# Residual sums as products with a scaled identity, and row norms shared between VectorE and ScalarE, in a four-layer transformer kernel

## The reference

```python
x = _layer_norm(DEEPNORM_ALPHA * x + mix, ln1_g[layer], ln1_b[layer])
ffn = _swiglu(x, ffn_w_gate[layer], ffn_w_up[layer], ffn_w_down[layer])
x = _layer_norm(DEEPNORM_ALPHA * x + ffn, ln2_g[layer], ln2_b[layer])
```

## Time and profile before

| | us |
|---|---|
| runs | 1052.35, 1056.54, 1061.19 |
| median | 1056.54 |
| the profiled execution | 1058.84 |
| its span | 1057.0 |
| PE busy | 994.2 (94%) |
| DVE busy | 655.3 (62%) |
| ACT busy | 452.5 (43%) |
| POOL busy | 155.5 (15%) |

### The profile page before, as it was taken

One profiled execution on the slowest core, in us unless ns is written; L12 is line 12 of the kernel. 1 busy time (PEld: TensorE's weight loads), 2 busy tenths in 40 slices (PEclk: granted clock), 3 DMA queues, 4 the chain that ended last, 5 costly groups with the idle time before them and its releaser, 6 DMA issues.

```text
span 1057.0 us, 15082 instructions
## 1 busy us (share of the span) xinstructions
PE 994.2 (94%) x5704; PEld 825.6 (78%) x5704; DVE 655.3 (62%) x1157; ACT 452.5 (43%) x689; POOL 155.5 (15%) x130
## 2 busy tenths in 40 slices
PE   5999989887999989999999999999999999999995
PEld 3899655676887668987788888878998778888884
DVE  4546453774674666655775766667446486766666
ACT  2253443632444623665334444443436334444441
POOL 3006001300691321140001000000006000000000
PEclk9999898998999999999999999999999999999998
DMA  9963354333553445321267544533533234654441
GB/s 376 351 241 136 123 197 159 121 120 130 188 197 141 163 178 196 130 82 47 113 225 252 219 179 179 189 145 137 198 128 121 84 124 167 243 197 179 179 179 40
DMA packets 23669, 178.40 MB, mean 169 GB/s; under 512 B 3743, under 2 KB 4175, under 8 KB 7111
## 3 DMA queue, kind: packets, MB, share of 16 engines
q1 hardware_dynamic: 19408, 166.70, 42.8%
q0 software_dynamic: 2224, 8.94, 2.5%
q10 hardware_dynamic: 1991, 2.14, 0.6%
HBM read 176.72 MB, written 1.05 MB: 168 GB/s over the span
## 4 chain that ended last, share of the span: by engine, by line
PE 83%; DVE 10%; DMA 4%; ACT 2%; issue 1%; POOL 0%; SPq 0%; DVEq 0%; ACTq 0%; POOLq 0%
PE G L958 14%; PE G L960 13%; PE G L959 13%; PE S L1062 7%; PE T L1062 7%; PE S L1061 3%; PE T L1061 3%; PE T L588 3%; PE T L483 2%; DVE wlo L1855 2%; PE G L407 1%; PE S L981 1%; PE G L604 1%; DMA ring<-in_ada_w 1%; PE G L602 1%; PE G L603 1%
## 5 line engine op out<-in xcount | busy, mean ns | idle before, releaser
L1972 DVE TENSOR_TENSOR wlo<-ring,whi 128x1024 fp32r<-128x1024 f32 (+1 forms) x90 | 154.5, 1722 | 91.3 <-ACT whi L1603 52.5
L958 PE MATMUL G<-whi,hTh 128*128 128x512 f32 (+3 forms) x560 | 199.9, 357 | 6.1 <-DVE hTl L524 3.4
L959 PE MATMUL G<-wlo,hTh 128*128 128x512 f32 (+3 forms) x544 | 187.6, 345 | 0.0
L960 PE MATMUL G<-whi,hTl 128*128 128x308 f32 (+3 forms) x496 | 168.7, 340 | 0.0
L1855 DVE TENSOR_TENSOR wlo<-ring,whi 128x1024 fp32r<-128x1024 f32 (+3 forms) x76 | 120.8, 1628 | 76.8 <-ACT whi L1498 76.5
L1062 PE MATMUL S<-hT,whi 128*128 128x512 f32 x352 | 128.1, 398 | 1.1 <-DVE wlo L1972 1.1
L1062 PE MATMUL T<-hT,whi 128*128 128x512 f32 x352 | 126.4, 394 | 0.0
L958 PEld LDWEIGHTS G<-whi,hTh 128*128 128x128 f32 x560 | 106.6, 190 | 20.1 <-DVE hTl L524 5.6
L1498 ACT CAST whi<-ring 128x1024 fp32r<-128x1024 f32 (+3 forms) x76 | 87.8, 1205 | 78.1 <-PE G L960 36.3
L959 PEld LDWEIGHTS G<-wlo,hTh 128*128 128x128 f32 x544 | 103.5, 190 | 9.3 <-issue 1.9
L960 PEld LDWEIGHTS G<-whi,hTl 128*128 128x128 f32 x496 | 94.1, 190 | 6.0
(11 more groups left out here) (334 smaller groups left out, 1762.8 us busy)
## 6 DMA issues: line engine op xcount, KB each, us to landing
ring<-in_ffn SPq DMA_DIRECT2D x44, 1536.0 KB, 6.4
ring<-in_ada_w SPq DMA_DIRECT2D x16, 1024.0 KB, 5.6
ring<-in_dil_w_in SPq DMA_DIRECT2D x16, 1024.0 KB, 4.8
ring<-in_cd_w_in SPq DMA_DIRECT2D x10, 1232.0 KB, 5.4
ring<-in_nsa_w_in SPq DMA_DIRECT2D x8, 1432.0 KB, 10.9
early<-in_ada_w SPq DMA_DIRECT2D x8, 1024.0 KB, 17.3
ring<-in_ab_w_in SPq DMA_DIRECT2D x4, 1440.0 KB, 6.2
vec<-in_vecs POOLq DMA_DIRECT2D x11, 512.0 KB, 5.2
```

Source lines behind the costliest of these rows:

```text
L958: pe.matmul(out_, act_h, w_h, start=first_, stop=False)
L959: pe.matmul(out_, act_h, w_l, start=False, stop=False)
L960: return pe.matmul(out_, act_l, w_h, start=False, stop=last_)
L1972: TT(wlo[b][:, part], ring[:, b, part], whi[b][:, part].bitcast(F32), ALU.subtract).then_inc(st[sig or what + "_lo"], 1)
```

## The change

All that follows is one change; nothing of what is computed is left out.

- **Residual of layers three and four.** In `project_out`, before the first weight item of a tile, PE puts ALPHA * x into that tile's two banks (`resid`), in place of one `keep_busy` product. DVE no longer adds; it takes the statistics from the banks, and the centring reads the banks in two halves.
- **First gate and up product.** It is made once for each token tile (`first_gate_up`): 32 passes of 256 columns, low weights against both parts of the activations. Tile 0's stands where four `keep_busy` products stood, and both `residual` products stand behind the transposes of tile 1.
- **Norms of layers one and two.** ACT squares the new x with a sum over the row (`row_squares`); DVE's three or four statistics instructions of a tile become one.
- **Norm after the feed-forward part.** Tile 1's mean and variance come from ACT, which reads the banks (`row_mean`, `row_spread`), while DVE works on tile 0.
- **Order.** The `late` blocks of layer one stand at p = 2, 5, 7, 9, 11, 12, the compressed products at 6, 8, 10, 13; the seventh `late` block stands before layer two's attention and the eighth at p = 2. The second weight item's low part of layer one's output is made in halves at p = 15 and before the last gate product. Layer two's second input item is multiplied with tile 0 before the transposes of tile 1. The three table loads wait for the 7th, 10th and 13th step of the first feed-forward part. POOL adds three branches before the last compressed sum. The scaled identity is made once, in another place (`cb`).

```diff
-        OUT_AT, LATE_AT, LATE_DIL = (6, 7, 10, 11), (2, 3, 5, 8, 9, 12), (2, 4)
+        OUT_AT, LATE_AT, LATE_DIL = (6, 8, 10, 13), (2, 5, 7, 9, 11, 12), (-1, 2)
...
+            if name in ("f0", "f1"):
+                return (TB[0], TB[1], S[1], TB[1])[g]
...
-            add_branch(1)
+            for q in range(1, 4):
+                add_branch(q)
             add_compressed(3)
-            for q in range(2, H // 2):
+            for q in range(4, H // 2):
                 add_branch(q)
...
-            for lo, base in ((0, P), (P, 0), (2 * P, P)):
+            for n, (lo, base) in enumerate(((0, P), (P, 0), (2 * P, P))):
+                pool.wait_ge(ffn[0]["act_ready"], 7 + 3 * n)
                 pool.dma_start(b8[:, :, lo:lo + P], bass.AP(tensor=rev.tensor, offset=base, ap=[[1, P], [rev.shape[1], 8], [1, P]])).then_inc(ck_loaded, 16)
...
+            def first_gate_up(name, st, t):
+
+                pe.wait_ge(*turned_tile(name, t))
+                pe.wait_ge(st["gu_lo"], 1)
+                for part, bank in enumerate((S[0], TB[0])):
+                    dst = bank[:, t * 2 * P:(t + 1) * 2 * P].rearrange("p (h c) -> p h c", h=2)
+                    for k in range(KT):
+                        at = slice((part * KT + k) * P, (part * KT + k + 1) * P)
+                        pe.matmul(dst, whi[0][:, at], hT2[:, k, :, t * P:(t + 1) * P], start=(k == 0), stop=False)
+                        ins = pe.matmul(dst, wlo[0][:, at], hT2[:, k, :, t * P:(t + 1) * P], start=False, stop=(k == KT - 1))
+                    if t == 1:
+                        ins.then_inc(st["gu_full"], 1)
+
...
-                gate_up(0, 0, True)
...
-                                             late_half == 0 and k == 0, late_half == 1 and k == OUT_K - 1)
+                                             i < 2 and late_half == 0 and k == 0, late_half == 1 and k == OUT_K - 1)
...
+                def resid(t):
+
+                    if i >= 2:
+                        pe.wait_ge(alpha_set, 1)
+                        for half in range(2):
+                            pe.matmul(G[OUT_BANK[half][t]][:], alpha_ident, x[:, t, half * 512:(half + 1) * 512], start=True, stop=False)
 
                 if not early:
                     turn_half(i, 0, *half_ready)
-                keep_busy(1, G[3])
+                if i < 2:
+                    keep_busy(1, G[3])
+                resid(0)
                 item(0, 0, 1).then_inc(used, 1)
                 pe.wait_ge(*all_ready)
+                resid(1)
                 if i == 1:
                     pe.wait_ge(shared_ready, 2)
...
+            dil_item(1, 1, 0, 0).then_inc(st["full"], 1)
             turn_pe(pe, "h1", norm_tiles(1), 1)
-            dil_item(1, 1, 0, 0).then_inc(st["full"], 1)
...
+            late_parts(pe, LATE_NSA, G[3])
             turn_pe(pe, "dil_rot", lambda g: pe.wait_ge(dil_s["rot_ready"], g + 1))
+            late_full(pe, LATE_NSA, G[3])
...
+                if p == 0:
+                    pe.wait_ge(late["taken"], LATE_NSA + 1)
...
+            first_gate_up("f0", ffn[0], 0)
+            turn_pe(pe, "f0", norm_tiles(5), 1)
             residual(0, 0, 11)
-            keep_busy(4)
-            turn_pe(pe, "f0", norm_tiles(5), 1)
             residual(0, 1, 12)
-            pe.wait_ge(*turned_all("f0"))
+            first_gate_up("f0", ffn[0], 1)
             ffn_pe("ffn0", ffn[0])
...
                 if name == "cd_in":
-                    high(name, 0, 1, KT * w)
+                    row_mean("ffn0")
                 turn_act(sc_e, turn_name, 0)
                 if name != "cd_in":
                     high(name, 0, 1, KT * w)
+                if name in ("dil_in", "ab_in"):
+                    row_squares(("dil_in", "ab_in").index(name), 1)
+                elif name == "cd_in":
+                    high(name, 0, 1, KT * w)
+                    row_spread(0)
                 turn_act(sc_e, turn_name, 1)
...
+            def row_squares(i, t):
+
+                sc_e.wait_ge(norm["resid"], 4 * i + 2 * (t + 1))
+                sc_e.activation(u[:, 0, 2 * D:3 * D], x[:, t, :], ACT.Square, scale=1.0 / 32, accum_out=var[:, t:t + 1]).then_inc(norm["squared"], 1)
+
+            def row_mean(name):
+
+                sc_e.wait_ge(used, split0[name] + FF_STEPS)
+                for half in range(2):
+                    ins = sc_e.activation(tok[:, 1, half * 512:(half + 1) * 512], G[2 + half][:], ACT.Copy, scale=1.0 / D,
+                                          accum_out=squares[:, half:half + 1])
+                ins.then_inc(norm["meaned"], 1)
+
+            def row_spread(i):
+
+                sc_e.wait_ge(norm["mean"], i + 1)
+                for half in range(2):
+                    ins = sc_e.activation(tok[:, 1, half * 512:(half + 1) * 512], G[2 + half][:], ACT.Square, scale=-1.0, bias=mv[:, 1, 0:1],
+                                          accum_out=squares[:, 2 + half:3 + half])
+                ins.then_inc(norm["squared"], 1)
+
...
+                if i < 2:
+                    row_squares(i, 0)
...
+            def squared_var(i, t):
+
+                dve.wait_ge(norm["squared"], NT * i + t + 1)
+                done(TS(var[:, t:t + 1], var[:, t:t + 1], EPS_RMS, None, ALU.add), norm["var"])
+
             def ada_norm(i, mod, t):
 
                 done(TT(tok[:, t, :], x[:, t, :], mod[:, D:2 * D], ALU.mult))
+                squared_var(0, t)
                 dve.wait_ge(norm["rstd"], 2 * i + t + 1)
...
 
                 moments([], t, pieces, True, EPS_LN)
-                done(STT(x[:, t, :], x[:, t, :], mv[:, t, 0:1], g, ALU.subtract, ALU.mult))
+                for half in range(2):
+                    cols = slice(half * 512, (half + 1) * 512)
+                    done(STT(x[:, t, cols], G[OUT_BANK[half][t]][:], mv[:, t, 0:1], g[:, cols], ALU.subtract, ALU.mult), outp["taken"])
                 dve.wait_ge(norm["rstd"], 2 * i + t + 1)
...
-                    if gatev is None:
-                        done(STT(part, part, ALPHA, y, ALU.mult, ALU.add), outp["taken"])
+                    if gatev is not None:
+                        done(TT(tmp[:, n % 2, :], y, gatev[:, cols], ALU.mult), outp["taken"])
+                        done(TT(part, part, tmp[:, n % 2, :], ALU.add), norm["resid"])
                     else:
-                        done(TT(tmp[:, n % 2, :], y, gatev[:, cols], ALU.mult), outp["taken"])
-                        done(TT(part, part, tmp[:, n % 2, :], ALU.add))
-                    done(dve.bn_stats(bstat[:, t, half, :], part))
+                        done(dve.bn_stats(bstat[:, t, half, :], y))
...
+                TT(wlo[b][:, part], ring[:, b, part], whi[b][:, part].bitcast(F32), ALU.subtract).then_inc(st[what + "_lo"], 1)
...
-                low_ffn(st, 0, 0, slice(KT * P, 2 * KT * P), "gu")
                 low_ffn(st, 0, 0, dn, "dn")
...
+                def center(t, half):
+
+                    cols = slice(half * 512, (half + 1) * 512)
+                    done(STT(x[:, t, cols], G[2 * t + half][:], mv[:, t, 0:1], g[:, cols], ALU.subtract, ALU.mult))
+
+                def mean_of_last():
+
+                    dve.wait_ge(norm["meaned"], i + 1)
+                    done(TT(mv[:, 1, 0:1], squares[:, 0:1], squares[:, 1:2], ALU.add), norm["mean"])
+
                 for t in range(NT):
 
                     if t == 0:
                         dve.wait_ge(ffn[i]["tile0"], 1)
+                        moments([G[half][:] for half in range(2)], 0, 2, True, EPS_LN)
+                        center(0, 0)
+                        center(0, 1)
+                        if turn_name is None:
+                            mean_of_last()
                     else:
-                        dve.wait_ge(used, split0[name] + FF_STEPS)
-                    moments([G[2 * t + half][:] for half in range(2)], t, 2, True, EPS_LN)
-                    for half in range(2):
-                        cols = slice(half * 512, (half + 1) * 512)
-                        done(STT(x[:, t, cols], G[2 * t + half][:], mv[:, t, 0:1], g[:, cols], ALU.subtract, ALU.mult))
+                        dve.wait_ge(norm["squared"], 2 * NT + i + 1)
+                        done(TT(mv[:, 1, 1:2], squares[:, 2:3], squares[:, 3:4], ALU.add))
+                        done(TS(var[:, 1:2], mv[:, 1, 1:2], 1.0 / D, EPS_LN, ALU.mult, ALU.add), norm["var"])
+                        center(1, 0)
+                        center(1, 1)
                     dve.wait_ge(norm["rstd"], 2 * n + t + 1)
                     scale_halves(n, b, t)
                     if t == 0 and turn_name is not None:
                         lows(0, (0,))
+                        mean_of_last()
                         turn_low(dve, turn_name, 0)
                         lows(0, (1,))
...
+                    low_out("nsa_out", 1, (0,))
...
+            low_out("nsa_out", 1, (1,))
...
+            late_sum(dve, LATE_NSA, G[3])
...
```

(5 more changed lines are left out.)

76 lines of the change are left out of this document (38 added, 38 removed).

## The result

The changed kernel took 1049.17 us (median of 20 runs, 1042.17 to 1056.42), the one before 1057.10 beside it (20 runs, 1051.65 to 1065.20). The ratio is 0.9924, 95% interval 0.9899 to 0.9948: 8 us faster where 14.5 were forecast. The forecast gave 0.69 to more than 1% faster; the measured 0.8% lies inside the 1% band, to which it gave 0.26. The profiled execution has a span of 1048.4 us, 8.6 under that of before, so its stages can account for the difference.

The account below looks back on a forecast made before the run. PE, busy 94% of the span, was taken as the bound. Eight terms summed to -15.4 us: from the profiled 1058.84 to 1043.4, less 2.3 for the median 1041.1, rounded up to 1042; range 1031 to 1051.

Parts of the forecast that it names:

- term 5: Layer three's input: low parts start earlier through a shorter norm and the slow stretch there goes, -1.6 us.
- terms 7 and 8: 7: spread table loads end a 1.14 us PE wait, -1.1 us; 8: shorter norm behind each feed-forward part, -1.3 and -1.4.
- term 6: Starts of the feed-forward parts: residual products and narrower gate and up passes add PE work, +1.05 us each, +2.1 together.
- Term 2: Layer one's output to layer two's input: shorter norm, earlier low part, idle time filled, slow stretch gone, -8.4 us.
- Term 1: Layer one's attention: ring wait at p = 3 goes, wait and slow stretch move from p = 9 to 12, -1.1 us.
- Terms 3 and 4: Layer two's attention: late block fills the kT wait, -1.0 us; at its end an earlier split removes the tok wait, -1.6.
- rival C: Slow stretches stay at the inputs of layers two and three, +3.4 and +1.2 us: 1047 us, chance 0.27.
- B: Layer one's slow stretch goes too, -5.1 us: 1037 us, chance 0.13.
- D: Float32 residual products and narrow passes at feed-forward starts run at 1.2 GHz, 29 us more: 1070 us, chance 0.05.
- E: The norms don't shorten; terms 2, 5 and 8 keep about a fifth: 1054 us, chance 0.05.

Follow-up runs that it names:

- resid_old: nsa_old with ALPHA * x added by DVE in the evictions of layers three and four, as before the change; 1042.21 us, ratio 0.9858 to the kernel before.
- stats_old: nsa_old with DVE's bn_stats, aggregate and scalars for the norms of layers one and two instead of ACT's squares; 1050.68 us, ratio 0.9944 to the kernel before.
- split_set: Changed kernel with POOL setting the low parts of layer two's first two output weight items to zero instead of subtracting; 1043.5 us, ratio 0.9881 to the kernel before.
- item_late: nsa_old with layer two's second input item multiplied with tile 0 behind tile 1's transposes, as before the change; 1048.17 us, ratio 0.9923 to the kernel before.
- gain_end: Changed kernel with DVE's scaling of layer two's modulation moved from p = 14 to behind p = 15; 1046.12 us, ratio 0.9879 to the kernel before.
- split_256: nsa_old with POOL's split subtractions made in pieces of 256 columns; 1040.17 us, ratio 0.9843 to the kernel before.
- nsa_old: Changed kernel with the order of layer one's attention, POOL's adds and one PE wait moved back; 1044.34 us, ratio 0.9896 to the kernel before.
- dil_mid: Changed kernel with layer two's eighth late block at p = 4 instead of 2, the seventh still ahead of the attention; ratio 0.9942 to the kernel before.
- best: split_256 with ALPHA * x added by DVE again, as in resid_old; 1039.57 us, ratio 0.9841 to the kernel before.

## Why the prediction was right in sign and wrong in size

**Measured as forecast:** term 5 (-1.6, measured -1.7), terms 7 and 8 (-2.4 together for layer three, measured -2.6, and -1.4 at the end, measured -1.3; no run takes 7 and 8 apart, but PE's wait of 1.14 us is gone), term 6 in layer three (+1.05, measured +1.3). Inside term 6 two errors cancel: the residual's own part was 3.44 - 0.91 = 2.5, and resid_old shows 1.65, so the first gate and up product and its idle products gave back less than the 1.5 I had. In layer four the stage got 0.3 shorter: the same 1.3 more, and a slow stretch of before (1.7 lost) that is absent, which nothing in the prediction foresaw. But term 5's working was wrong: stats_old shows 0.1 us for the norm's length there. The 1.7 are the slow stretch, which both profiles with the old norm have and no other. PE's wait for the low parts did shrink from 1.80 to 0.36, and a wait of 1.39 for x ahead of tile 1's transposes took its place.

**Term 2, too high by 1.5 us.** The chain worked out: tile 1 starts 6.9 us earlier, and 8.0 where no slow stretch reaches in from the attention (36.23 us in split_set, with the same code there). (Its products began at 252.12 before, not at 252.68: the first overlaps the idle product.) Its shares were not as I wrote them. Taken back one by one, the norm's length holds about 1 and not 2.8, the low part 0.3 and not 1.4, the order of item 1 1.2. The kernel before loses 3.4 between 236 and 252 us; stats_old and item_late each lose 1.7 there and the other eleven profiles nothing. That leaves about 2 us of the 8.0 that no single part holds.

**Term 1 failed.** The step "the wait and the slow stretch move from p = 9 to p = 12 and keep their size" held for that stretch (3.4 instead of 5.1 lost). What I left out is what the compressed product at p = 13 does to its neighbour: POOL's addition beside DVE's scaling at p = 14, probs 2.40 us late, and 6.6 us of clock behind it. gain_end shows the first link, from the scaling to the late probs; the second, to the clock, it only makes likely. I had listed the places of the blocks and not what DVE runs at p = 13 and 14.

**Terms 3 and 4 failed.** "I keep the gain, since PE is not waiting for DVE there" was the step. PE was not waiting in most iterations, but a DVE product that takes 1.2 to 1.4 us more makes it wait, four times, 3.96 us in all, and then 3.4 are lost to the clock. Without the clock's 3.4 the two terms are -1.1 instead of -2.6. split_set and split_256 show the mechanism. The Trainium skill, "SBUF — State Buffer", section "SBUF: two separate sides", has the very rule: of a DVE product with two SBUF inputs and a POOL instruction that reads SBUF, the one that comes second is blocked for the other's whole instruction. The trace agrees: DVE's product ends 0.3 us behind POOL's subtraction at 353 and 357 us, and pieces of 0.7 us end most of the harm. I had weighed it at 1.6 us and dismissed it.

**What the 7 us are.** The sum was -15.4, and 4.6 of it was clock given back at the inputs of layers two and three. Over all executions it gave back 0.2, with an error of 0.9. So more than half of the miss is that the prediction followed each slow stretch of before to its end and put no term for new ones, though it lists waits of their size that stay. That 1049 lies inside the range is in part luck: the range ran up to 1051 to take in rival C, and what filled it is clock loss at places that are not C's.

**The rivals.** B didn't come: the stretch of the block at p = 12 is there, 3.4 lost. C was wrong at both its places (1.00 in both windows), but slow stretches of the same size came at two others. D and E didn't come. On the clock, the Trainium skill, "TensorE: Matmul & The Clock Gate", section "Why this matters for your kernels", has the clock hold as long as PE has no long idle gaps. The two longest waits, 5.71 us before and 5.17 in item_late, do have a stretch behind them. But the others at 1.2 GHz, up to the last 10 us of the span, stand in or behind single waits of 0.8 to 2.4 us, so the traces disagree with it as a bound.

**Left open:** what decides whether the clock falls behind a given wait (nsa_old has 1.30 us ahead of 168 and no stretch, item_late 1.31 and one). The same code has the stretch in some executions and not in others, and no run here tells them apart.

## What to carry to other kernels

- When a POOL instruction with long operands moves to where DVE works for a bound engine, cut it into short pieces, here 0.7 us instead of 2.35; the sum of the pieces may be longer and the kernel faster.
- Before moving a block in a hand-woven loop, write down what each engine runs in the two iterations around its new place; cost moved work by its neighbours and not by its own length.
- Compare stages of the profile, with the clock loss of each beside it, and the same two shares over all executions: here the clock's share ran from 10 to 22 us between kernels, and moved work saved 2.6 us and cost 6.9 of it.

## What was not expected of the hardware

- A 128x256 DVE product with both inputs in SBUF ended 0.27 to 0.29 us behind the POOL instruction in which it started, a subtraction or a cast. It took 1.54 to 2.21 us instead of 0.42 where 1.3 us or more of a 128x1024 subtraction was left, and up to 0.91 (dil_mid) in a cast.
- Thirteen of the fourteen profiles have at least one slow stretch between 138 us and layer three's input; best has none, and all have the one near 120 us.
- ACT's Square with a row sum took 1.06 us for 1024 columns and 0.19 to read the sum.
